# Ordering the gate and up projections of a mixture-of-experts unit: all gate steps ahead of all up steps

## The chip, the cores and the metric

The kernel runs on one core of one Trainium2 chip. The metric is the device time of one execution in microseconds. The kernel before was timed three times, and one more execution was taken with the hardware profiler. All arithmetic that matters here is 32-bit.

## The reference

One inference step of a decoder with two layers, for a prompt of 512 tokens and 8 sampled tokens (520 rows of 1024 features). Each layer adds attention and a convolution branch, and then a mixture of experts. Only the second half is touched by the change:

```python
def hier_moe(h, w_rg, w_re, w_gate, w_up, w_down):
    ...                     # routing: every token gets 2 of 16 experts, all of one group of four
    hg = jnp.einsum('nd,edf->nef', x, w_gate)      # d = 1024, f = 512, e = 16 experts
    hu = jnp.einsum('nd,edf->nef', x, w_up)
    act = jax.nn.silu(hg) * hu * gates[..., None].astype(x.dtype)
    y = jnp.einsum('nef,efd->nd', act, w_down)
```

The kernel computes this sparsely: for each expert it gathers the rows routed to it, up to 128 of them, and adds the result back to those rows.

## The kernel before, in words

**Work and units.** Each layer runs attention, convolution and the output projection, then routing, then the experts. The 16 experts are put in an order by their number of rows. Ten of them form units of their own with 128 places for rows; the last six by size are joined two and two into three paired units (numbers 2, 6 and 11, `PAIRED`), each expert with 64 places. So there are 13 units (`UNITS`), numbered 0 to 12, in each of two layers: 26 in all. `places_of(u)` gives the one or two experts of a unit, and `halves_of(u)` the rows of the tile that each takes. In a paired unit the two experts' matmuls use different halves of TensorE's columns.

**Weights.** Each expert has three weight matrices, gate (j = 0), up (j = 1) and down (j = 2), of 2048 KB each. SyncE loads them into nine slots, in one fixed order (`loads_in_order`, L91): for a single unit gate, up, down; for a paired unit gate and up of the first expert, gate and up of the second, then both downs. Load number n goes to slot n modulo 9 (`slot_of`). Slots 0 to 5 are in the tile `ring`; slot 6 is named `w_last`, 7 `x` and 8 `feat` in the trace, since these tiles are used again. SyncE's loop (L560 to L572) takes the loads strictly in this order; `unit` (L485) waits on `slot_used` of the slot (L489 or L492, L491 being a register step between) until TensorE has made its last use of the previous contents, and then issues the transfer (L493), which adds 16 to `slot_in` when it lands. A load whose slot is not free holds back all loads behind it.

**TensorE** (L971 to L1035) works through the units in an order written out by hand:

```python
for u in range(UNITS):
    if u + 1 < UNITS:
        gate_up(u + 1, range(4))
    turn_hidden(u)
    if u + 1 < UNITS:
        gate_up(u + 1, range(4, KC))
    if u + 2 < UNITS:
        gathered(u + 2)
    down(u)
```

`gate_up(u, ks)` (L971) multiplies the unit's transposed rows `xe_t` with the gate and the up matrix: for each of the 8 chunks k, first gate, then up. Gate results accumulate in PSUM bank 2 or 4, up results in bank 3 or 5, by the unit's parity (banks 2 and 3 are called `pair` in the trace, 4 and 5 `bank`). Ahead of chunk 0 it waits for `xt_ok` (the transposed rows) and for all gate and up loads of the unit (`landed`, L966). Behind chunk 7 stands a matmul of one row and one column (L987) into bank 7 that adds 1 to `gu_ps`; it is called the mark below. The last gate matmul and the last up matmul each give their slot free. `turn_hidden(u)` (L990) transposes the hidden rows of the unit before (4 transposes, L602), `gathered(u + 2)` (L955) transposes the gathered rows of the unit after (8 transposes, L602), and `down(u)` (L996) multiplies by the down matrix and ends with a mark of its own (L1013). For unit 0, `gate_up` is cut into single chunks, with a `unit_list` (L946, small matmuls that make the lists of rows) behind each.

**ScalarE**, for each unit, in this order: `hidden_out(u)` (L1288) copies the transposed hidden rows out of PSUM; `silu(u + 1)` (L1284) waits for `gu_ps` and computes silu of the gate bank into `hid`; `y_half(u)` (L1293) waits for the mark of `down(u)` and scales half of the result.

**VectorE**, for each unit: `hidden(u)` (L1938) waits for `silu_ok` and multiplies `hid` by the up bank (L1408, `v_rows<-v_rows,...`); `features(u + 2)` (L1916) scales the transposed rows of the next unit but one; `y_half(u)` (L1943) waits for the mark of `down(u)` and scales the other half (L1946).

**GpSimd** issues the gather of each unit's rows (L1357) and the scatter-add of its results (L1368).

The functions as they stand in the kernel before:

Of the kernel before, what the change touches and what calls it, by code (L numbers as in the profile page):

```python
# [31 lines left out]
KC = D // P  # L32
# [16 lines left out]
F = 512  # L49
# [9 lines left out]
UNITS = SINGLES + (EXPERTS - SINGLES) // 2  # L59
# [12 lines left out]
def places_of(u):  # L72

    q = u + sum(1 for pair in PAIRED if pair < u)
    return [q, q + 1] if u in PAIRED else [q]
# [15 lines left out]
def loads_in_order():  # L91

    return [(q, j) for u in range(UNITS) for js in ((0, 1), (2,)) for q in places_of(u) for j in js]


def slot_of(q, j):

    return loads_in_order().index((q, j)) % SLOTS_MOE


def load_of(q, j):

    n = loads_in_order().index((q, j))
    return n // SLOTS_MOE + (1 if n % SLOTS_MOE < SLOTS else 0)


def loads_of(s):

    return sum(1 for q, j in loads_in_order() if slot_of(q, j) == s) + (1 if s < SLOTS else 0)
# [85 lines left out]
def hybrid_step(nc, a, o, x_rows, xn_rows):  # L195
# [17 lines left out]
    with ExitStack() as ctx:  # L213
# [3 lines left out]
        def sem(name):  # L217
            return ctx.enter_context(nc.semaphore(name))
# [13 lines left out]
        def cs(name, rows=P):  # L232
            at, width = where[name]
            return const[0:rows, at:at + width]
# [27 lines left out]
        xe_t = probs_flat.rearrange("p (s c n) -> p s c n", s=2, n=P)  # L262
# [64 lines left out]
        bank = [pair_bank[i // 2][:, i % 2, :] for i in range(4)]  # L327
# [7 lines left out]
        slot_used = [sem(f"slot_used{s}") for s in range(SLOTS_MOE)]  # L335
        order_ok = sem("order_ok")
        slots = [ring[:, s, :] for s in range(SLOTS)]
# [89 lines left out]
        xe_in = [sem("xe_in0"), sem("xe_in1")]  # L427
        xt_ps = sem("xt_ps")
        xt_ok = sem("xt_ok")
        gu_ps = sem("gu_ps")  # L430
        silu_ok = sem("silu_ok")
        hid_ok = sem("hid_ok")
# [34 lines left out]
        def halves_of(u):  # L467

            return [slice(0, HALF), slice(HALF, P)] if u in PAIRED else [slice(0, P)]
# [129 lines left out]
        def _(pe):  # L599
            def turn(dst, src, rows):  # L600

                return pe.transpose(dst, src, ident[0:rows, 0:rows])  # L602

            def paired(row, chunk):

                at = (chunk // 2) * 2 * P + chunk % 2
                return row[:, at:at + 2 * P - 1:2]

            pe.wait_ge(start_in, 48)
            with pe.Fori(0, DEPTH) as l:  # L610
# [4 lines left out]
                for c in range(CH):  # L615
                    mm = turn(bank[1][:, c * TAPS:(c + 1) * TAPS], conv_w_rows[:, c * P:(c + 1) * P], TAPS)
                mm.then_inc(vec_ps, 1)

                for t in range(TILES):
                    pe.wait_ge(xn_ok, l * TILES + t + 1)  # L620
                    for g in range(2):
                        b = 4 + 2 * (t % 2) + g
# [4 lines left out]
                        for c in range(4):  # L627
                            mm = turn(bank[b][:, c * P:c * P + rows_of[t]],
                                      x[0:rows_of[t], t, (4 * g + c) * P:(4 * g + c + 1) * P], rows_of[t])
# [4 lines left out]
                for c in range(CH):  # L634
                    if c >= 2:
                        pe.wait_ge(u_ok, l * CH + c - 1)
                    for half in range(2):
# [3 lines left out]
                        for k in range(KC):  # L641
                            w = ring[:, half, k * AW + c * P:k * AW + (c + 1) * P]
                            pe.matmul(main[:, :], w, feat[:, k, 0:SEQ], start=(k == 0), stop=(k == KC - 1))  # L643
                            mm = pe.matmul(smp, w, feat[:, k, SEQ:TOK], start=(k == 0), stop=(k == KC - 1))  # L644
# [10 lines left out]
                for c in range(CH):  # L655
                    for j in range(2):
                        mm = pe.matmul(bank[7][:, c * DEC + 4 * j:c * DEC + 4 * j + 4],
                                       state[:, j, c * P:(c + 1) * P], cs("in_seq", 4 * BUF), start=True, stop=True)
# [273 lines left out]
                for later in range(1, TILES + 1):  # L932
                    mm = pe.matmul(bank[7][:, later * EXPERTS:width + EXPERTS], ones,
                                   chosen[:, 0:(TILES + 1 - later) * EXPERTS], start=False, stop=True,
                                   skip_group_check=True)
# [10 lines left out]
                def unit_list(u):  # L946

                    pe.wait_ge(hot_ok, l * LISTS + FIXED + u + 1)
                    for t in range(TILES):
                        for rows in halves_of(u):  # L950
                            mm = pe.matmul(bank[0][rows, u * PAY:(u + 1) * PAY], hot[:, u % 2, t, rows], pay[:, t, :],
                                           start=(t == 0), stop=(t == TILES - 1))
                    mm.then_inc(idx_ps, 1)

                def gathered(u):  # L955

                    b = u % 2
                    if u >= 2:
                        pe.wait_ge(ht_ok, l * UNITS + u - 1)
                    pe.wait_ge(xe_in[b], l * 16 * len(range(b, UNITS, 2)) + 16 * (u // 2 + 1))  # L960
                    for g in range(2):
                        for c in range(4):
                            mm = turn(bank[6 + g][:, c * P:(c + 1) * P], paired(xe[:, b, :], 4 * g + c), P)
                        mm.then_inc(xt_ps, 1)

                def landed(q, j):  # L966

                    s = slot_of(q, j)
                    pe.wait_ge(slot_in[s], l * 16 * loads_of(s) + 16 * (load_of(q, j) + 1))

                def gate_up(u, ks):  # L971
                    b = u % 2
                    if ks[0] == 0:
                        pe.wait_ge(xt_ok, l * 2 * UNITS + u * 2 + 2)
                        for q in places_of(u):
                            for j in range(2):
                                landed(q, j)
                    for k in ks:
                        for j in range(2):
                            for q, rows in zip(places_of(u), halves_of(u)):  # L980
                                s = slot_of(q, j)
                                mm = pe.matmul(bank[2 + 2 * b + j][rows, :], xe_t[:, b, k, rows],  # L982
                                               slots[s][:, k * F:(k + 1) * F], start=(k == 0), stop=(k == KC - 1))
                                if k == KC - 1:
                                    mm.then_inc(slot_used[s], 1)
                    if ks[-1] == KC - 1:
                        pe.matmul(bank[7][0:1, 0:1], ones[:, 0:1], ones[:, 0:1], start=True, stop=True)\  # L987
                            .then_inc(gu_ps, 1)

                def turn_hidden(u):  # L990
                    pe.wait_ge(hid_ok, l * UNITS + u + 1)
                    for c in range(FC):
                        mm = turn(bank[6][:, c * P:(c + 1) * P], hid[:, u % 2, c * P:(c + 1) * P], P)
                    mm.then_inc(ht_ps, 1)
# [24 lines left out]
                for u in range(FIXED):  # L1019
                    unit_list(u)  # L1020
                for k in range(KC):
                    gate_up(0, range(k, k + 1))
                    unit_list(FIXED + k)
                for u in range(FIXED + KC, UNITS):
                    unit_list(u)
                gathered(1)
                for u in range(UNITS):
                    if u + 1 < UNITS:
                        gate_up(u + 1, range(4))
                    turn_hidden(u)  # L1030
                    if u + 1 < UNITS:
                        gate_up(u + 1, range(4, KC))
                    if u + 2 < UNITS:
                        gathered(u + 2)
                    down(u)  # L1035
# [6 lines left out]
                with pe.If(n_spill > 0):  # L1042
                    pe.wait_ge(y_ok, l * 2 * UNITS + 2 * UNITS + 1)
                    pe.sem_inc(pe_tick, 1)
                    with pe.Fori(0, n_spill) as i:
                        m = pe.snap(before + i)
                        pe.wait_ge(sp_hot, m + 1)
                        for t in range(TILES):
                            mm = pe.matmul(bank[0][:, 0:PAY], hot[:, 0, t, :], pay[:, t, :],
                                           start=(t == 0), stop=(t == TILES - 1))  # L1050
                        mm.then_inc(sp_idx, 1)
                        pe.wait_ge(sp_xe, m * 16 + 16)
                        for g in range(2):
                            for c in range(4):
                                mm = turn(bank[6 + g][:, c * P:(c + 1) * P], paired(xe[:, 0, :], 4 * g + c), P)
# [3 lines left out]
                        for k in range(KC):  # L1059
                            for j in range(2):  # L1060
                                mm = pe.matmul(bank[2 + j][:, :], xe_t[:, 0, k, :], ring[:, j, k * F:(k + 1) * F],
                                               start=(k == 0), stop=(k == KC - 1))
                        mm.then_inc(sp_gu, 1)
                        pe.wait_ge(sp_hid, m + 1)
                        for c in range(FC):
                            mm = turn(bank[6][:, c * P:(c + 1) * P], hid[:, 0, c * P:(c + 1) * P], P)
                        mm.then_inc(sp_ht, 1)
                        pe.wait_ge(sp_htok, m + 1)
                        for k in range(FC):
                            for j in range(2):  # L1070
                                mm = pe.matmul(bank[j][:, :], hid_t[:, 0, k, :],
                                               ring[:, 2, k * D + j * F:k * D + (j + 1) * F],
                                               start=(k == 0), stop=(k == FC - 1))
# [5 lines left out]
        def _(act):  # L1079
# [5 lines left out]
            with act.Fori(0, DEPTH) as l:  # L1085
# [196 lines left out]


                def silu(u):  # L1284
                    act.wait_ge(gu_ps, l * UNITS + u + 1)
                    act.activation(hid[:, u % 2, :], bank[2 + 2 * (u % 2)][:, :], ACT.Silu).then_inc(silu_ok, 1)

                def hidden_out(u):  # L1288
# [4 lines left out]
                def y_half(u):  # L1293
                    act.wait_ge(dn_ps, l * UNITS + u + 1)
                    if u == 0:
# [3 lines left out]
                        .then_inc(y_ok, 1)  # L1299

                silu(0)
                for u in range(UNITS):
                    hidden_out(u)
# [102 lines left out]
        def _(v):  # L1406
            def tt(out, in0, in1, op):
                return v.tensor_tensor(out, in0, in1, op)  # L1408
# [24 lines left out]
            with v.Fori(0, DEPTH) as l:  # L1433
# [26 lines left out]
                for t in range(TILES):  # L1460
                    n = rows_of[t]
                    for g in range(2):
                        v.wait_ge(turn_ps, l * 10 + 2 * t + g + 1)
                        b = bank[4 + 2 * (t % 2) + g][:, :].rearrange("p (c n) -> p c n", c=4)[:, :, 0:n]
# [473 lines left out]
                def hidden(u):  # L1938
                    b = u % 2
                    v.wait_ge(silu_ok, l * UNITS + u + 1)  # L1940
                    tt(hid[:, b, :], hid[:, b, :], bank[3 + 2 * b][:, :], ALU.mult).then_inc(hid_ok, 1)

                def y_half(u):  # L1943
# [106 lines left out]
```

## Time and profile before

| | |
|---|---|
| median of 3 runs | 1523.86 us (1518.89 to 1526.81) |
| the profiled execution, its own time | 1521.59 us |
| its span, first to last instruction | 1519.8 us |
| TensorE busy | 1302.7 us, 86% of the span |
| VectorE / ScalarE / GpSimd busy | 626.5 / 233.3 / 152.4 us |
| mean granted TensorE clock | 0.919 of full speed |
| bytes moved | 318.98 MB, mean 210 GB/s |
| expert units of layer 0 / layer 1, from the first gate matmul to the last down matmul | about 434 to 749 us / 1184 to 1500 us |

"Busy" is the union of an engine's instructions. Each 32-bit matmul shows as two records in the trace, so "x16" at a matmul line is 8 matmuls of a single unit; in a paired unit it is 4 chunks' worth per expert half, and 32 records take the time of 16. PE is TensorE, PEld its weight loads, DVE VectorE, ACT ScalarE, POOL GpSimd, SP SyncE; a "q" behind an engine marks its queue. Names such as `probs`, `v_rows` and `qk_t` are tiles that the expert stage uses again under other names: `xe_t` lies in `probs`, `hid` and `hid_t` in `v_rows`, the gathered rows and `ye` in `qk_t`.

### The profile page before, as it was taken

What the parts mean: (1) busy time and instruction counts of PE and PEld (TensorE: products, weight loads), DVE (VectorE), ACT (ScalarE), POOL (GpSimd) and SP (SyncE); (2) the same over time, 40 slices, a digit from 0 to 9 for tenths busy, and PEclk for the clock granted to TensorE, in tenths of its full rate; (3) what the DMA queues carried; (4) which work ended last, traced back from release to release, by engine and by line L of the source; (5) the groups of instructions that cost most, each with busy time, mean ns of one, the idle gap of its engine ahead of it and who ended that gap; (6) DMA issues with size and microseconds to landing.
All of it is one profiled execution on the core that took longest, in us unless ns stands there. A gap on an engine that the chain in (4) does not pass through costs nothing.

```text
span 1519.8 us, 15302 instructions
## 1 busy us (share of the span) xinstructions
PE 1302.7 (86%) x4730; PEld 629.9 (41%) x4730; DVE 626.5 (41%) x1260; ACT 233.3 (15%) x736; POOL 152.4 (10%) x80
## 2 busy tenths in 40 slices
PE   1999985689769999999649999759895799999994
PEld 1553443445333443444235444335453344444441
DVE  2469988542363111111035799865415611101100
ACT  2002132231100000000020113233211000000000
POOL 0000242000001111110100022400000001101001
PEclk9999997799879999999869999867997799999997
DMA  7800234267355999999384013333742859989973
GB/s 248 309 0 23 70 97 138 67 219 290 113 208 184 357 381 344 374 385 341 63 290 183 0 51 102 92 104 96 285 188 101 309 184 350 386 321 389 388 271 91
DMA packets 102113, 318.98 MB, mean 210 GB/s; under 512 B 10488, under 2 KB 11058, under 8 KB 101932
## 3 DMA queue, kind: packets, MB, share of 16 engines
q1 hardware_dynamic: 84066, 275.49, 48.6%
q0 software_dynamic: 8048, 26.35, 7.2%
q10 hardware_dynamic: 9914, 16.09, 3.2%
q8 instruction: 42, 0.69, 0.2%
q14 instruction: 43, 0.35, 0.1%
HBM read 294.88 MB, written 33.87 MB: 216 GB/s over the span
## 4 chain that ended last, share of the span: by engine, by line
PE 56%; DVE 17%; DMA 12%; DVEq 7%; issue 4%; ACT 1%; ACTq 1%; SPq 1%; POOL 0%; POOLq 0%
PE pair L982 12%; PE pair L1008 9%; PE bank L982 8%; PE pair L643 8%; PE pair L889 8%; DMA w_last<-in_w_up 5%; DVE conv L1504 4%; DVEq L1506 3%; PE bank L602 3%; DMA ring<-in_w_up 3%; DVE probs L1408 2%; DVE sc_dec L1565 2%; DMA x_rows<-qk_t,rows_g 2%; DVE conv L1488 1%; PE pair L762 1%
## 5 line engine op out<-in xcount | busy, mean ns | idle before, releaser
L982 PE MATMUL pair<-ring,probs 128*128 128x512 f32 (+1 forms) x384 | 167.7, 623 | 9.3 <-DMA w_last<-in_w_up 6.9
L1408 DVE TENSOR_TENSOR probs<-bank,vec_g 128x512 f32<-128x512 f32 x52 | 33.5, 685 | 307.2 <-PE bank L602 306.8
L982 PE MATMUL bank<-ring,probs 128*128 128x512 f32 (+1 forms) x352 | 145.0, 606 | 7.7 <-DVE probs L1408 5.6
L643 PE MATMUL pair<-feat,ring 128*128 128x512 f32 x256 | 141.8, 647 | 2.2 <-DVE feat L1408 2.2
L674 PE MATMUL pair<-ring,feat 128*128 128x512 f32 (+1 forms) x320 | 136.9, 606 | 1.6 <-ACT v_rows L1145 1.6
L1008 PE MATMUL pair<-ring,v_rows 128*128 128x512 f32 (+1 forms) x320 | 130.3, 605 | 1.5 <-ACT v_rows L1290 1.5
L1341 POOL TENSOR_TENSOR w_last<-x 128x2048 f32<-128x2048 f32 x16 | 74.0, 4641 | 401.4 <-ACT x L1180 296.2
L1504 DVE SCALAR_TENSOR_TENSOR conv<-u_t,conv_w,conv 128x512 f32<-128x512 f32 x120 | 105.4, 919 | 5.2 <-issue 0.9
L1946 DVE TENSOR_SCALAR qk_t<-pair,gate 128x512 f32<-128x512 f32 x26 | 19.5, 751 | 200.6 <-PE bank L1013 103.5
L1368 POOL DMA_INDIRECT x_rows<-qk_t,rows_g x32 | 49.6, 1552 | 514.4 <-DVE qk_t L1946 468.8
L1488 DVE SCALAR_TENSOR_TENSOR conv<-u_t,conv_w,conv 128x512 f32<-128x512 f32 x120 | 90.2, 751 | 17.3 <-issue 13.2
L982 PEld LDWEIGHTS pair<-ring,probs 128*128 128x128 f32 (+1 forms) x384 | 61.3, 178 | 77.9 <-issue 70.5
L982 PEld LDWEIGHTS bank<-ring,probs 128*128 128x128 f32 (+1 forms) x352 | 57.4, 180 | 80.6 <-issue 79.2
L674 PE MATMUL bank<-ring,feat 128*128 128x512 f32 (+1 forms) x160 | 81.1, 604 | 0.0
L674 PEld LDWEIGHTS pair<-ring,feat 128*128 128x128 f32 (+1 forms) x320 | 50.6, 171 | 73.1 <-issue 72.3
L1008 PEld LDWEIGHTS pair<-ring,v_rows 128*128 128x128 f32 (+1 forms) x320 | 53.1, 183 | 66.0 <-issue 65.8
L644 PEld LDWEIGHTS bank<-feat,ring 128*128 128x128 f32 x256 | 49.5, 194 | 63.2 <-issue 63.2
L1357 POOL DMA_INDIRECT qk_t<-xn_rows,rows_g x26 | 27.3, 1050 | 435.2 <-DVE rows_g L1854 369.3
L889 PE MATMUL pair<-w_last,feat 128*128 128x512 f32 (+1 forms) x160 | 64.8, 592 | 0.0
L889 PE MATMUL pair<-ring,feat 128*128 128x512 f32 (+1 forms) x160 | 64.2, 597 | 0.0
L1008 PE MATMUL pair<-feat,v_rows 128*128 128x512 f32 (+1 forms) x128 | 56.4, 594 | 0.0
L602 PE MATMUL bank<-const,probs 128*128 128x128 f32 x144 | 27.5, 315 | 29.6 <-DVE probs L1639 29.6
(269 smaller groups left out, 1596.2 us busy)
## 6 DMA issues: line engine op xcount, KB each, us to landing
ring<-in_w_gate SPq DMA_DIRECT2D x24, 2048.0 KB, 21.0
ring<-in_w_up SPq DMA_DIRECT2D x22, 2048.0 KB, 21.6
ring<-in_w_down SPq DMA_DIRECT2D x20, 2048.0 KB, 13.2
ring<-in_w_in SPq DMA_DIRECT2D x10, 2048.0 KB, 17.9
x<-in_cache_k SPq DMA_DIRECT2D x64, 256.0 KB, 3.1
x<-in_cache_v SPq DMA_DIRECT2D x64, 256.0 KB, 2.9
feat<-in_w_down SPq DMA_DIRECT2D x8, 2048.0 KB, 20.7
w_last<-in_w_gate SPq DMA_DIRECT2D x6, 2048.0 KB, 15.6
```

Of the source, the lines that this page charges most:

```text
L602: return pe.transpose(dst, src, ident[0:rows, 0:rows])
L643: pe.matmul(main[:, :], w, feat[:, k, 0:SEQ], start=(k == 0), stop=(k == KC - 1))
L644: mm = pe.matmul(smp, w, feat[:, k, SEQ:TOK], start=(k == 0), stop=(k == KC - 1))
L674: mm = pe.matmul(dst[j][rows_at(t, j), :], feat[:, k, cols(t)], ring[:, 2 + j, k * AW:(k + 1) * AW], start=(k == 0), stop=(k == KC - 1))
L889: mm = pe.matmul(bank[2 * (t % 2) + j][rows_at(t, j), :], feat[:, k, cols(t)], w[:, (k % 4) * D + j * AW:(k % 4) * D + (j + 1) * AW], star ...
L982: mm = pe.matmul(bank[2 + 2 * b + j][rows, :], xe_t[:, b, k, rows], slots[s][:, k * F:(k + 1) * F], start=(k == 0), stop=(k == KC - 1))
L1008: mm = pe.matmul(bank[j][rows, :], hid_t[:, b, k, rows], slots[s][:, k * D + j * F:k * D + (j + 1) * F], start=(k == 0), stop=(k == FC - 1))
L1341: pool.tensor_tensor(qk_prod[:, half, :, :], pages[:, half * 4:half * 4 + 4, :], q_rep[:, half:half + 1, :].to_broadcast([P, PAGES, AW]), ...
L1368: pool.indirect_dma_start(out=x_rows[:, :], out_offset=bass.IndirectOffsetOnAxis(ap=rows_g[0:n, at:at + 1], axis=0), in_=ye[0:n, b, :], in ...
L1408: return v.tensor_tensor(out, in0, in1, op)
L1488: v.scalar_tensor_tensor(acc, u_t[:, c, bass.ds(w, SEQ)], conv_w[:, c, bass.ds(w, 1)], acc, ALU.mult, ALU.add)
L1504: v.scalar_tensor_tensor(conv[:, k, 0:SEQ], u_t[:, k, bass.ds(w, SEQ)], conv_w[:, k, bass.ds(w, 1)], conv[:, k, 0:SEQ], ALU.mult, ALU.add)
```

## The change

`gate_up(u, ks)` becomes `gate_or_up(u, j, ks)`, which does the eight chunks of one projection alone. TensorE runs all gate chunks of unit u + 1, then `turn_hidden(u)`, then all up chunks of unit u + 1. Each of the two ends with a mark: the gate's adds to a new semaphore `gate_ps`, the up's to `gu_ps`. The gate part waits for `xt_ok` and for the gate loads, the up part for the up loads. `silu` waits for `gate_ps`; `hidden` on VectorE waits for `silu_ok` and also for `gu_ps`. In unit 0 the eight pieces between the lists are now two gate chunks each for the first four and two up chunks each for the last four. The order of the loads and the waits of SyncE are unchanged.

```diff
+        gate_ps = sem("gate_ps")
         gu_ps = sem("gu_ps")
...
-                def gate_up(u, ks):
+                def gate_or_up(u, j, ks=range(KC)):
                     b = u % 2
                     if ks[0] == 0:
-                        pe.wait_ge(xt_ok, l * 2 * UNITS + u * 2 + 2)
+                        if j == 0:
+                            pe.wait_ge(xt_ok, l * 2 * UNITS + u * 2 + 2)
                         for q in places_of(u):
-                            for j in range(2):
-                                landed(q, j)
+                            landed(q, j)
                     for k in ks:
-                        for j in range(2):
-                            for q, rows in zip(places_of(u), halves_of(u)):
-                                s = slot_of(q, j)
-                                mm = pe.matmul(bank[2 + 2 * b + j][rows, :], xe_t[:, b, k, rows],
-                                               slots[s][:, k * F:(k + 1) * F], start=(k == 0), stop=(k == KC - 1))
-                                if k == KC - 1:
-                                    mm.then_inc(slot_used[s], 1)
+                        for q, rows in zip(places_of(u), halves_of(u)):
+                            s = slot_of(q, j)
+                            mm = pe.matmul(bank[2 + 2 * b + j][rows, :], xe_t[:, b, k, rows],
+                                           slots[s][:, k * F:(k + 1) * F], start=(k == 0), stop=(k == KC - 1))
+                            if k == KC - 1:
+                                mm.then_inc(slot_used[s], 1)
                     if ks[-1] == KC - 1:
                         pe.matmul(bank[7][0:1, 0:1], ones[:, 0:1], ones[:, 0:1], start=True, stop=True)\
-                            .then_inc(gu_ps, 1)
+                            .then_inc(gu_ps if j else gate_ps, 1)
...
                 for k in range(KC):
-                    gate_up(0, range(k, k + 1))
+                    gate_or_up(0, k // 4, range(2 * k % KC, 2 * k % KC + 2))
                     unit_list(FIXED + k)
...
                     if u + 1 < UNITS:
-                        gate_up(u + 1, range(4))
+                        gate_or_up(u + 1, 0)
                     turn_hidden(u)
                     if u + 1 < UNITS:
-                        gate_up(u + 1, range(4, KC))
+                        gate_or_up(u + 1, 1)
...
                 def silu(u):
-                    act.wait_ge(gu_ps, l * UNITS + u + 1)
+                    act.wait_ge(gate_ps, l * UNITS + u + 1)
...
                 def hidden(u):
                     b = u % 2
                     v.wait_ge(silu_ok, l * UNITS + u + 1)
+                    v.wait_ge(gu_ps, l * UNITS + u + 1)
```

## Rows read from the trace of the kernel before

**Rows 1.** Section 2 of the page: busy tenths and granted clock in 40 slices.
```profile
PE   1999985689769999999649999759895799999994
PEclk9999997799879999999869999867997799999997
DMA  7800234267355999999384013333742859989973
```

**Rows 2.** The chain in order of time, unit 6 of both layers: start us, us, what.
```profile
551.59 25.49 DMA w_last<-in_w_up
577.13 8.78 PE pair L982 x32
586.50 7.02 PE pair L982 x32
...
1328.00 8.78 PE pair L982 x32
```

**Rows 3.** Line 982 in a stretch: us, PE busy, PEld busy, clock, DMA share, GB/s.
```profile
577.00:586.00 9.00, 8.78 (x32) 2.61 (x32) 0.81 1.04 355
```

**Rows 4.** TensorE's waits, 430 to 755 us (layer 0): total us, times, longest.
```profile
PE pair L982 <- DMA w_last<-in_w_up: 3.6, 1, 3.6
PE bank L602 <- DVE v_rows L1408: 1.5, 1, 1.5
PE bank L982 <- DMA w_last<-in_w_up: 0.5, 1, 0.5
```

**Rows 5.** TensorE's waits, 1180 to 1505 us (layer 1): total us, times, longest.
```profile
PE pair L982 <- DMA w_last<-in_w_up: 3.3, 1, 3.3
PE bank L982 <- DMA ring<-in_w_up: 0.9, 1, 0.9
PE bank L982 <- DMA w_last<-in_w_up: 0.6, 1, 0.6
PE pair L982 <- DMA ring<-in_w_up: 0.2, 1, 0.2
```

**Rows 6.** TensorE's timeline, unit 4 of layer 0: start us, us, instruction, records.
```profile
534.25 1.02 PE L982 MATMUL pair<-x,probs 128*128 128x512 f32 x2
535.11 0.60 PE L602 MATMUL bank<-const,v_rows 128*128 128x128 f32 x4
...
541.56 1.02 PE L982 MATMUL pair<-x,probs 128*128 128x512 f32 x2
542.51 0.19 PE L987 MATMUL bank<-const 128*1 128x1 f32 x2
542.63 1.23 PE L602 MATMUL bank<-const,qk_t 128*128 128x128 f32 x8
```

**Rows 7.** SyncE's own waits over the whole span: total us, times, longest.
```profile
SPq L492 <- PE pair L1008: 318.7, 22, 30.4
SPq L492 <- PE pair L982: 40.3, 4, 20.1
```

**Rows 8.** Line 493, 550.9 to 551.4 us: second gate load of unit 6, layer 0.
```profile
L493 SPq DMA_DIRECT2D ring<-in_w_gate x1: 373/373/373, 551.0 to 551.0; - x1
DMA to landing us min/median/max: 21.0/21.0/21.0
```

**Rows 9.** Line 493, 574.7 to 575.2 us: gate load of unit 7, layer 0.
```profile
L493 SPq DMA_DIRECT2D ring<-in_w_gate x1: 373/373/373, 574.8 to 574.8; - x1
DMA to landing us min/median/max: 21.3/21.3/21.3
```

**Rows 10.** Line 493, 1302.1 to 1302.7 us: second gate load of unit 6, layer 1.
```profile
L493 SPq DMA_DIRECT2D ring<-in_w_gate x1: 373/373/373, 1302.2 to 1302.2; - x1
DMA to landing us min/median/max: 20.6/20.6/20.6
```

**Rows 11.** VectorE's timeline around the end of a down projection, layer 0.
```profile
528.34 0.75 DVE L1946 TENSOR_SCALAR qk_t<-pair,gate 128x512 f32<-128x512 f32 x1 [6.43 <-PE pair L1013]
529.01 0.68 DVE L1408 TENSOR_TENSOR v_rows<-v_rows,bank 128x512 f32<-128x512 f32 x1
```

## The prediction

> **What bounds the kernel now.** I first read the slices [rows 1]. In both expert stages (the second run of nines in the PE line, and the last) TensorE is busy nine tenths or more almost without a break, at full granted clock but for single slices. The DMA engines are close behind: nine tenths in most of the same slices. So the stage is TensorE's, with a weight supply that has little to spare, and a change pays there only if it takes idle or slow time from TensorE itself. The chain of waits [rows 2] then shows where the supply does win: at unit 6, a paired unit, it leaves TensorE for the transfer of the second up matrix, issued at 551.59 and landed at 577.1. The gate-and-up half behind it takes 8.78 us; the next one, the same work, takes 7.02. TensorE's waits [rows 4, 5] give all such places. In layer 0: 3.6 us (unit 6) and 0.5 (unit 11). In layer 1: 3.3 (unit 6), 0.9, 0.6 and 0.2. Every one of them names an **up** load. That is what the change can act on, since it lets gate chunks run without the up matrix.
>
> **Removed: the waits for up loads.** They sum to 3.6 + 0.5 + 3.3 + 0.9 + 0.6 + 0.2 = 9.1 us. After the change TensorE needs only the gates at that point. At unit 6 of layer 0 it starts at 577.1 after a wait of 3.6 us, so it is ready at 573.5 [rows 2, 4]; the later of the two gates was issued at 551.0 and landed 21.0 us later, at 572.0 [rows 8]. In layer 1 it is ready at 1328.0 − 3.3 = 1324.7 [rows 2, 5], less the 0.9 us saved before it, and the gate landed at 1302.2 + 20.6 = 1322.8 [rows 10]. Both are in time, all the more as the new marks (below) delay TensorE by 6 × 0.21 = 1.3 us up to there. The up chunks follow 7.0 us of gate chunks and 0.6 us of transposes later, about 582 in layer 0, against a landing at 577.1. The other four waits are below 1 us, and 7 us of gate chunks cover them. I take all 9.1 us.
>
> **Removed: slow matmuls behind the idle.** The 8.78 us against 7.02 [rows 2] is the price of the wait in unit 6: TensorE had stood idle 3.6 us, and over its next half the granted clock is 0.81 of full speed [rows 3], a part at 1.2 GHz and the rest at 2.4. That is 1.76 us. Behind the wait of 3.3 us in layer 1 the same half takes 8.78 us too [rows 2], so the same 1.76. The short waits show no such loss that I can separate. Together 3.5 us. Gross gain: 12.6 us.
>
> **Added: a second mark in every unit.** 26 marks (13 units, 2 layers). From the start of the last matmul to the first transpose behind it takes 535.11 − 534.25 = 0.86 us without a mark and 542.63 − 541.56 = 1.07 us with one [rows 6]. A mark thus costs 0.21 us of TensorE, not hidden by anything, and 26 cost 5.5 us. The lower bound is the step from mark to transpose alone, 542.63 − 542.51 = 0.12 us or 3.1 us in all; the upper one is 0.25 us each, 6.5 in all, since readings to 0.01 us at four places may be off by 0.04. I take 5.5, since it is measured between the very neighbours that the new mark gets. The Trainium skill, "TensorE: Matmul & The Clock Gate", section "Back-to-back issue gap", puts a matmul of 1 to 64 columns at about 25 ns when warm; a mark of two records would then cost an estimated 0.05 us, 26 of them 1.3 us, and the net gain would be 11.3 us. The row above disagrees with that.
>
> **Moved: the order of the matmuls.** Gate and up alternated between two PSUM banks; now 8 chunks in a row accumulate in one bank. No row shows two such instructions in a row. The nearest is inside one matmul: its two records go to the same bank, and end 1.02 us after its start, while the next instruction starts after 0.86 [rows 6]. At an even pace that is a record every 0.43 us, each 1.02 − 0.43 = 0.59 long, overlapping the next by 0.16 us within a bank as between banks. No turnaround shows, so I take zero; the upper bound is a rival below. The number of weight loads is the same, each record having its own before and after. A gain is excluded, as the matmuls already follow at their streaming rate.
>
> **Moved: when slots come free.** The gate slots are freed some 7.6 us earlier, one half of the unit. But SyncE issues strictly in order, and it hardly ever waits for gate-and-up: 318.7 us over 22 waits stand on down (L1008), 40.3 us over 4 on L982, two of them 20 us long [rows 7]. Those two are the first reuse of unit 0's gate slot in each layer, by a load of unit 2 that TensorE reaches only after all of unit 1, and the load behind it needs the up slot, free as late as before. I cost this at nothing. The up slots are freed 0.21 us later per mark, already in the sum. No DMA issue is moved on any queue, and POOL's gathers and scatters depend on events (`xt_ps`, `y_ok`) behind the same work as before.
>
> **Moved: silu.** It can start about 7.7 us earlier. Its consumer, the multiply, stands on VectorE behind `y_half` of the unit before, which waits for that unit's down: the L1946 row is followed at once by the multiply [rows 11]. Down comes after both gate and up, so the multiply starts when it did. The same holds at the end of a layer, where TensorE's 1.5 us wait for the multiply [rows 4] stays. Worth nothing. The new wait of VectorE on `gu_ps` is long satisfied there. Behind TensorE's wait for the up loads stand the gather's transposes and down, hence SyncE's next load; with 5 us to spare in unit 6 nothing of it is late.
>
> **What is late next.** TensorE reaches unit 7 sooner while the loads already queued do not. From unit 6's first chunk to unit 7's, TensorE now needs 8.78 + 7.02 us of gate and up [rows 2], 7.0 of down (as many matmuls as one half) and 0.6 + 1.2 of transposes [rows 6], 24.6 in all; without the slow part and with one more mark it is 23.0 us, so from 574.8 (573.5 + 1.3) it ends at 597.8. Unit 7's gate, issued at 574.8, lands at 596.1 [rows 9]: 1.7 us to spare. The loads behind it are issued at the end of down and move forward with TensorE.
>
> **The sum.** −9.1 − 3.5 + 5.5 = −7.1 us against the profiled 1521.59, giving 1514.5 there. The median of the three runs stands 2.3 us above the profiled execution, so the predicted median is 1523.86 − 7.1, or 1516.8 us.
>
> **The rivals.**
>
> 1. *The mark is cheaper.* If most of its 0.21 us is overlap that the next instruction takes back, the lower bound of 3.1 us holds and the gain is 9.5: 1514.4 us. For it: the two readings are of one unit, and the transposes on either side differ in their tiles. Against it: both intervals run between starts of real work, with no wait in them. Chance 0.16.
>
> 2. *The waits move instead of going.* The supply has only 1 to 3 us to spare at units 6 and 7. If the gates land late there, TensorE idles again and its clock may fall again. With 1 us of idle and 1.76 us of slow chunks back in each layer, 5.5 us of the gain is lost: 1522.3 us. For it: the DMA line at nine [rows 1], landings that depend on gathers beside them. Against: both gates were down before TensorE arrived [rows 8, 10]. Chance 0.20.
>
> 3. *Accumulating in one bank costs a turnaround,* the rival on the slower side. Its place is each of the 14 same-bank neighbours of a unit: 24 units × 14, and 8 in each of the two units 0, 352 in all. If each had to let the one before drain, it would lose that overlap of 0.16 us, 56 us in all: 1573 us. It decides from 7.1 / 352 = 20 ns per neighbour; 42 ns make it slower by over 0.5%. For it: these pairs are in no row. Against: the two records of a matmul pay nothing. Chance 0.06.
>
> 4. *The change does not do what it says.* The gate does not in fact start early, since something else holds it (the rows' `xt_ok`, or a gate that lands last). Then only the marks remain: 1529.4 us. Rows 8 and 10 speak against it. Chance 0.04.
>
> **How the numbers follow.** The forecast has the remaining 0.54. A measurement of this kernel can tell about 0.5%, 7.6 us, from no change, so "faster" is below 1516.2 and "slower" above 1531.5. The forecast value lies almost on the first line: of its 0.54 I give 0.25 to faster, 0.29 to same. Rival 1 gives 0.14 and 0.02; rival 2 0.02 and 0.18; rival 3 0.01 to same and 0.05 to slower; rival 4 0.03 to same and 0.01 to slower. That is 0.41 faster, 0.53 same, 0.06 slower. The range starts below rival 1 by the spread that three runs show (1518.89 is 5 us under the median), less part of it since it is a median: 1511.0. It reaches past rival 2: 1523.5. That leaves out rivals 3 and 4 and the tails.
>
> **What would show it.** Right: TensorE's waits on `in_w_up` in the expert stages are gone or below 0.5 us; both halves of unit 6 take about 7.0 us; 52 marks instead of 26 on gate and up; from the last gate matmul to the transposes 1.07 us; the L1946 row still followed at once by the multiply; SyncE's waits still on down. Wrong: waits on `in_w_gate` in units 6 to 9 and a clock that falls again there (rival 2); gate chunks further than 0.86 us apart (rival 3); a multiply that starts ahead of `y_half`, which would give silu's early start a value that I deny it.

## The result, and the profile after

| | before | changed |
|---|---|---|
| median, 8 runs each | 1523.14 us (1518.55 to 1526.81) | 1513.31 us (1508.68 to 1517.11) |
| ratio of the two, 95% interval | | 0.9935, 0.9918 to 0.9952 |
| the profiled execution, own time / span | 1521.59 / 1519.8 us | 1517.11 / 1515.3 us |
| mean granted TensorE clock, profiled | 0.919 | 0.914 |

The change is worth 9.8 us on the medians, 0.65%; the interval reaches from 7.3 to 12.5 us. The forecast was 1516.8 us in a range of 1511.0 to 1523.5, a gain of 7.1. The profiled execution of the changed kernel is the slowest of its eight, so the two spans are only 4.5 us apart; lengths below are therefore compared stage by stage. The mean clock of the profiled execution is not higher either: it rises in the expert stages (0.97 to 0.98) and is lower in the first 435 us (0.91 to 0.89), which the change does not touch.

The slices of the page, same three lines as [rows 1]:

```profile
PE   1999986799868999999649999858896799999994
PEclk9999996599969999999969999966997799999997
DMA  8800234177363999999375012332752849999973
```

The picture is the same: TensorE and the DMA engines are both near nine tenths in the expert stages. It can't show what changed. TensorE's waits can. Layer 0 (430 to 755 us), the answer to [rows 4]; the columns are total us, times, longest:

```profile
PE bank L603 <- DMA qk_t<-xn_rows,rows_g: 6.7, 1, 6.7
PE bank L982 <- DVE probs L1408: 3.0, 1, 3.0
PE pair L952 <- DVE conv L1408: 1.7, 3, 0.9
PE bank L603 <- DVE v_rows L1408: 1.5, 1, 1.5
PE pair L982 <- DVE probs L1408: 1.0, 1, 1.0
PE pair L1008 <- ACT v_rows L1290: 0.8, 1, 0.8
```

This is the whole list, and no weight load is in it (idle below 0.15 us is not listed). Layer 1's list has none either: all 9.1 us of [rows 4, 5] are gone. The wait of 1.5 us for the multiply in the last unit is still there, as forecast.

The chain at unit 6 of layer 0, the answer to [rows 2]; start us, us, what:

```profile
574.91 2.58 PE pair L1008 x6
577.48 0.12 PE pair L1013 x2
577.61 7.02 PE pair L982 x32
584.62 0.12 PE bank L987 x2
584.74 0.59 PE bank L603 x4
585.33 7.02 PE pair L982 x32
592.35 0.12 PE bank L987 x2
```

No DMA is in the chain, down is followed by the gate chunks at once, and both halves take 7.02 us where the first took 8.78. The granted clock over that stretch (here line 982 in 577 to 586 us, columns as [rows 3]) is 1.00 where it was 0.81:

```profile
577.00:586.00 9.00, 7.83 (x36) 2.55 (x38) 1.00 1.04 382
```

The marks, the answer to [rows 6], from TensorE's timeline in unit 4 of layer 0:

```profile
531.72 7.13 PE L982 MATMUL pair<-w_last,probs 128*128 128x512 f32 x16
538.79 0.19 PE L987 MATMUL bank<-const 128*1 128x1 f32 x2
538.91 0.66 PE L603 MATMUL bank<-const,v_rows 128*128 128x128 f32 x4
539.40 7.03 PE L982 MATMUL pair<-x,probs 128*128 128x512 f32 x16
546.36 0.19 PE L987 MATMUL bank<-const 128*1 128x1 f32 x2
546.48 1.23 PE L603 MATMUL bank<-const,qk_t 128*128 128x128 f32 x8
```

Eight chunks in one bank take 7.03 us, as eight alternating ones did: no turnaround. The transposes start 1.07 us behind the start of the last gate matmul, as forecast (eight chunks at 0.86 us: the last one starts at 537.84). But the chunks behind them follow after 539.40 − 538.91 = 0.49 us. In the kernel before it was 535.55 − 535.11 = 0.44, by [rows 6] and the row that follows there:

```profile
535.55 1.02 PE L982 MATMUL pair<-w_last,probs 128*128 128x512 f32 x2
```

So 0.05 us of a mark's price stands behind the transposes, where the forecast did not look.

SyncE still waits on down, 296.3 us over 22 waits, and 41.6 us over 4 on gate and up: the gate slots that come free earlier start no load earlier that TensorE waits for.

```profile
SPq L493 <- PE pair L1008: 296.3, 22, 30.7
SPq L493 <- PE pair L982: 41.6, 4, 13.4
```

The next load, unit 7's gate (line 494, 578.7 to 579.2 us, the answer to [rows 9]):

```profile
L494 SPq DMA_DIRECT2D ring<-in_w_gate x1: 373/373/373, 578.9 to 578.9; - x1
DMA to landing us min/median/max: 21.0/21.0/21.0
```

It landed at 599.9 and TensorE asked for it at 600.5. I had given it 1.7 us to spare; it had 0.6. The working had delayed TensorE by the new marks but left the issue at its old time, 574.8. The issue follows the end of unit 5's down by 1.4 us in both kernels (573.4 and 574.8 before, 577.5 and 578.9 here), so it moves with the marks too.

The same length of work can be read between the ends of two units' down matmuls in the timelines. In us, layer 0 / layer 1; "with unit 6" is the stretch that holds unit 6's gate and up, "last two units" runs from the end of down of unit 10 to that of unit 12, and the expert stage from the first gate matmul to the end of the last down:

```
kernel                          single unit   with unit 6      last two units   expert stage
before, first profile           22.64         28.29 / 27.92    33.57 / 33.81    315.1 / 316.9
before, second profile          22.64         28.85 / 27.63    33.58 / 33.72    317.5 / 316.8
changed, first profile          22.91         23.01 / 23.01    32.10 / 33.79    311.7 / 312.9
changed, second profile         22.91         23.01 / 23.01    32.10 / 32.10    311.8 / 311.9
```

### The profile page after: what moved, and what is told of

It is laid out like the page before. It is cut to its first block, busy times and chain, and to the rows that moved or that the text cites. A ratio compares the mean times of both kernels' runs of the same rounds, so it can differ in the third digit from the quotient of the medians.

```text
span 1515.3 us, 15414 instructions
## 1 busy us (share of the span) xinstructions
PE 1312.0 (87%) x4782; PEld 632.1 (42%) x4782; DVE 626.7 (41%) x1260; ACT 230.4 (15%) x736; POOL 152.5 (10%) x80
## 4 chain that ended last, share of the span: by engine, by line
PE 64%; DVE 17%; DVEq 7%; DMA 4%; issue 4%; ACT 1%; ACTq 1%; SPq 0%; POOL 0%; POOLq 0%
PE pair L982 13%; PE bank L982 11%; PE pair L1008 11%; PE pair L644 8%; PE pair L890 8%; PE bank L603 4%; DVE conv L1504 4%; DVEq L1506 3%; DVE probs L1408 2%; DVE sc_dec L1565 2%; DMA x_rows<-qk_t,rows_g 2%; DVE conv L1488 1%; PE pair L763 1%; PE pair L766 1%; DVE u_t L1408 1%
## 5 line engine op out<-in xcount | busy, mean ns | idle before, releaser
L982 PE MATMUL pair<-ring,probs 128*128 128x512 f32 (+1 forms) x384 | 163.2, 611 | 1.9 <-DVE probs L1408 1.9
L1408 DVE TENSOR_TENSOR probs<-bank,vec_g 128x512 f32<-128x512 f32 x52 | 33.5, 685 | 299.7 <-PE bank L603 299.3
L1298 ACT ACTIVATE qk_t<-pair,gate 128x512 f32<-128x512 f32 x26 | 17.9, 687 | 355.2 <-PE pair L1013 187.2
```

## The experiments

Each kernel is timed against the kernel before on the same chip; ratios are to it.

**e4_before_again and e7_changed_again: second profiles.** No edit.

> The kernel before once more, for a second profile of it. I forecast a gain of 7.1 us from the first profile and 9.8 was measured on the medians. If the first profile showed smaller waits than usual, this one shows more than 9.1 us of TensorE's waits for up loads; if not, 9 us again, and the rest is in the clock or in other stages.

> The changed kernel once more, for a second profile. If the stage of the experts again takes 311 to 313 us in each layer with no wait for a load, then the changed kernel's steady length is known and the rest of the difference lies in how long the kernel before waits; if the last unit again takes 32.1 us in layer 0 against 33.5 before, that part is the change's too and not chance.

Measured: the second profile of before has TensorE waiting 4.2 and 1.0 us in layer 0, 3.0, 1.2 and 0.6 in layer 1 for up loads:

```profile
PE pair L982 <- DMA w_last<-in_w_up: 4.2, 1, 4.2
PE bank L982 <- DMA w_last<-in_w_up: 1.0, 1, 1.0
```

That is 10.0 us against 9.1, so the first profile was a little mild. The second profile of the changed kernel has no wait for a load. Two profiles each give expert stages of 633.1 us before and 624.2 after, both layers together: 9.0 us, close to the 9.8 of the medians. These two second profiles are single executions (1526.21 and 1517.53 us). The last two units are 1.5 to 1.7 us shorter in three of four stages of the changed kernel.

**e3_gate_waits_for_up: everything but the early start.**

```diff
                         for q in places_of(u):
                             landed(q, j)
+                            if j == 0:
+                                landed(q, 1)
```

> The changed kernel, but the gate chunks wait for the up loads too. Everything else (order of the matmuls, two marks, silu on the gate's mark, gate slots freed early) is as in the changed kernel. Theory: the waits come back (unit 6: 3.5 less 1.8 us of marks ahead of it, so about 2 us in each layer, with or without slow chunks behind), and the time is that of the kernel before with two marks: 1525 to 1527 us, ratio 1.002. Rival (the gain is from the order, from silu or from slots freed early): 1513 us, ratio 0.9935.

Measured: 1524.36 us, ratio 1.0012 (0.9997 to 1.0027). The waits are back, here layer 0's:

```profile
PE pair L984 <- DMA w_last<-in_w_up: 3.2, 1, 3.2
PE bank L984 <- DMA ring<-in_w_up: 0.3, 1, 0.3
```

This one added wait undoes the whole gain. Order, silu on the gate's mark and the earlier freeing of gate slots are all still in, and are worth nothing together that these runs can see. I had expected about 2 us of wait at unit 6, from 3.5 less the marks ahead of it; it was 3.2 and 2.5.

**e2_before_two_marks: the marks alone.**

```diff
+        gate_ps = sem("gate_ps")
...
-                    if ks[-1] == KC - 1:
+                    if ks[-1] in (KC // 2 - 1, KC - 1):
                         pe.matmul(bank[7][0:1, 0:1], ones[:, 0:1], ones[:, 0:1], start=True, stop=True)\
-                            .then_inc(gu_ps, 1)
+                            .then_inc(gu_ps if ks[-1] == KC - 1 else gate_ps, 1)
```

> The kernel before with a second mark, for which nothing waits, behind chunk 3 of every gate-and-up. Theory: 26 x 0.26 = 6.8 us more work on TensorE, of which the waits for up loads at unit 6 swallow the 7 marks ahead of them in each layer (3.6 us): 1523.1 + 3.2, about 1526.3 us, ratio 1.002; single units 22.9 us. Rival (a mark is nearly free): ratio 1.000, single units 22.65 us.

Measured: 1524.38 us, ratio 1.0016 (1.0002 to 1.0029); single units take 22.91 us, and unit 6 waits 2.9 and 2.6 us. The marks cost what their number says, and part of it disappears in the waits, which are shorter than in the kernel before. e2 and e3 give the same time: with the same marks and the same waits, alternating banks or not makes no difference beyond their intervals of about 2 us each way. So the turnaround is at most about 10 ns for each of the 352 neighbours, and the chunks' 7.03 us in both orders leave less.

**e1_one_mark: the early start without its mark.**

```diff
-                    if ks[-1] == KC - 1:
+                    if ks[-1] == KC - 1 and j == 1:
                         pe.matmul(bank[7][0:1, 0:1], ones[:, 0:1], ones[:, 0:1], start=True, stop=True)\
-                            .then_inc(gu_ps if j else gate_ps, 1)
+                            .then_inc(gu_ps, 1)
...
-                    act.wait_ge(gate_ps, l * UNITS + u + 1)
+                    act.wait_ge(gu_ps, l * UNITS + u + 1)
...
-                    v.wait_ge(gu_ps, l * UNITS + u + 1)
```

> The changed kernel without the gate's mark; silu waits for gu_ps again, as before the change. Theory (the gain is the early start of the gate chunks, the mark is a pure cost, silu's early start is worth nothing): a single unit in the changed profile takes 22.91 us against 22.64 before, so a mark costs 0.26 us, 26 of them 6.8 us; this kernel should take 1513.3 - 6.8 = 1506.5 us, ratio to before 0.989, with no wait of TensorE for an up load. Rival (silu's early start carries part of the gain): 1513 us or more, ratio 0.9935 or above.

Measured: 1510.45 us, ratio 0.9907 (0.9888 to 0.9926). By the ratios it is 4.3 us faster than the changed kernel, between my 6.8 and the rival's nothing. Single units are back at 22.64 us. Two things took the rest. A first wait for a gate load shows, unit 7's, 0.2 us in layer 0 and 0.3 in layer 1:

```profile
PE bank L982 <- DMA ring<-in_w_gate: 0.2, 1, 0.2
```

And the last two units took 33.5 us in both layers, not 32.1.

**e5_silu_on_slot: silu early, without a mark.**

```diff
-                    act.wait_ge(gate_ps, l * UNITS + u + 1)
+                    for q in places_of(u):
+                        act.wait_ge(slot_used[slot_of(q, 0)], used_after(q, 0, l))
```

The gate's mark is left out as in e1_one_mark, so TensorE's part is the same; `used_after` is the number that the slot's semaphore has reached after that load's last use.

> The changed kernel without the gate's mark, but with silu still early: it waits for the semaphore by which the last gate matmul frees its slot. TensorE does what it does in e1_one_mark, and only silu's start differs. Theory (silu's early start is worth nothing, since the multiply stands behind y_half on VectorE): the time of e1_one_mark within noise, ratio 0.990 to 0.991, and the multiply starts 0.7 us after y_half as before. Rival (silu's early start gains something): 0.988 or lower.

Measured: 1510.35 us, ratio 0.9912 (0.9892 to 0.9931), the same as e1_one_mark. The timelines show why. ScalarE's silu of one unit (L1293; start us, us):

```profile
533.93 0.59 ACT L1293 ACTIVATE v_rows<-pair 128x512 f32<-128x512 f32 x1
```

and the next two rows of VectorE that matter:

```profile
548.67 0.75 DVE L1954 TENSOR_SCALAR qk_t<-pair,gate 128x512 f32<-128x512 f32 x1 [6.28 <-PE bank L1019]
549.34 0.68 DVE L1415 TENSOR_TENSOR v_rows<-v_rows,pair 128x512 f32<-128x512 f32 x1
```

silu is done at 534.5, and the multiply that uses it starts at 549.3, straight behind `y_half` (L1954), which waited for the mark of down. The 15 us between are idle for the result.

**e6_no_marks: no marks at all.** As e5_silu_on_slot, and

```diff
-                    if ks[-1] == KC - 1:
-                        pe.matmul(bank[7][0:1, 0:1], ones[:, 0:1], ones[:, 0:1], start=True, stop=True)\
-                            .then_inc(gu_ps if j else gate_ps, 1)
...
-                    pe.matmul(bank[2 + 2 * b][0:1, 0:1], ones[:, 0:1], ones[:, 0:1], start=True, stop=True)\
-                        .then_inc(dn_ps, 1)
...
-                    v.wait_ge(dn_ps, l * UNITS + u + 1)
+                    for q in places_of(u):
+                        v.wait_ge(slot_used[slot_of(q, 2)], used_after(q, 2, l))
```

with the same replacement in the multiply (load 1), in ScalarE's `y_half` (load 2) and in SyncE's wait ahead of a spill.

> As e5_silu_on_slot, and the marks of up and of down are gone too: the multiply and both y_half wait for the slot semaphores that the last up and last down matmul add to. Theory: a mark costs about 0.26 us, so a single unit takes 22.1 us instead of 22.64 and 52 marks are worth 13 us. But one mark less per unit already made TensorE wait 0.2 to 0.3 us for the gate of unit 7; 7 units x 0.53 us sooner must meet that load again, so 2.5 to 4 us of wait for a gate load come back in each layer, perhaps with slow chunks behind them. Net 3 to 8 us below e1_one_mark: 1503 to 1507 us, ratio 0.985 to 0.989. Rival (marks are free, or the supply follows): ratio 0.991, or 0.982 with no wait.

Measured: 1502.56 us, ratio 0.9855 (0.9834 to 0.9877), a version that beats both kernels. Single units take 21.99 us. The supply is met where I said, in layer 0 at units 7 and 6:

```profile
PE bank L988 <- DMA ring<-in_w_gate: 1.3, 1, 1.3
PE pair L988 <- DMA ring<-in_w_gate: 1.1, 1, 1.1
```

and in layer 1 for 1.3 and 0.4 us. That is 2.4 and 1.7 us in the two layers, a little less than the 2.5 to 4 I had expected. With 4.1 us of wait in all, no slow chunks follow: unit 7's first half shows 7.13 us in the timeline.

```profile
598.61 7.13 PE L988 MATMUL bank<-ring,probs 128*128 128x512 f32 x16 [1.28 <-DMA ring<-in_w_gate]
```

**e9_before_no_marks: no marks, old order.** The same replacements in the kernel before.

> The kernel before (gate and up chunk by chunk, all loads waited for ahead of them) without its 52 marks, the waits taken from the slot semaphores as in e6_no_marks. Theory (the supply at unit 6 limits this order): single units take 22.1 us, but the marks ahead of unit 6, 6 units x 0.5 us, are given back there as a longer wait for the up load, 6 to 7 us in each layer instead of 3.5; also more wait in units 11 and 3. Of 13 us some 6 to 8 are kept: 1515.5 to 1517.5 us, ratio 0.995 to 0.996, that is, about 12 us above e6_no_marks although both lack all marks. Rival (supply is no limit): ratio 0.991.

Measured: 1521.62 us, ratio 1.0004 (0.9988 to 1.0020). I expected to keep 6 to 8 of the 13 us; the interval leaves room for 1.8 us at most. TensorE's waits in layer 0:

```profile
PE pair L988 <- DMA w_last<-in_w_up: 4.7, 1, 4.7
PE bank L988 <- DMA w_last<-in_w_up: 2.8, 1, 2.8
PE bank L988 <- DMA ring<-in_w_up: 1.1, 1, 1.1
PE pair L988 <- DMA ring<-in_w_up: 0.7, 1, 0.7
```

and 8.2 us in layer 1: 17.5 us in all against 9.1 in [rows 4, 5]. The clock falls further too. Around unit 6 of both layers, columns as [rows 3], first the kernel before (line 982), then this one (line 988); these windows hold the wait as well:

```profile
573.00:583.00 10.00, 5.87 (x20) 1.89 (x22) 0.83 1.04 370
1324.00:1334.00 10.00, 6.00 (x20) 1.89 (x22) 0.83 1.04 373
573.00:583.00 10.00, 3.73 (x10) 1.25 (x12) 0.68 1.03 385
1322.00:1332.00 10.00, 5.62 (x16) 1.77 (x18) 0.66 1.04 358
```

The stretch with unit 6 takes 29.5 us where the same work without waits takes 22.65 (e8_gates_first): 4.7 us of wait and 2.1 behind it. The one with unit 11's gate and up takes 27.2 us in layer 0. Added up over the ten stretches from the end of unit 0's down to the end of unit 10's, both layers, this kernel takes 469.6 us and the kernel before 467.6 and 468.5 (two profiles): nothing of the marks' time is kept there. Its expert stages as a whole are 628.7 us, 4.4 less than before, and the last two units are 4.2 us shorter (31.4 and 31.7 us; more on these below); the timed runs do not show these 4.4 us, and why is open.

**e8_gates_first: both gates of a pair loaded first.** As e6_no_marks, and

```diff
-    return [(q, j) for u in range(UNITS) for js in ((0, 1), (2,)) for q in places_of(u) for j in js]
+    return [(q, j) for u in range(UNITS) for js in ((0,), (1,), (2,)) for q in places_of(u) for j in js]
```

> As e6_no_marks, and the loads of a paired unit come in the order gate, gate, up, up, down, down, so that TensorE's first part needs the first two loads of the unit and not the first and third. Theory: e6_no_marks waits 1.1 and 0.4 us for the second gate of unit 6, and this wait goes; the 1.3 us in each layer for the gate of unit 7 stays or grows by what was saved, since it stands behind all six loads of unit 6. So 0 to 2 us below e6_no_marks: ratio 0.984 to 0.986. Rival (the order of loads decides all waits): all waits for gates gone, ratio 0.982.

Measured: 1501.65 us, ratio 0.9881 (0.9856 to 0.9906), its interval overlapping that of e6. I had expected 0.984 to 0.986, below e6; no gain over e6 is shown, and the two ratios are from different chips. The wait at unit 6 is gone and the one at unit 7 has taken it up:

```profile
PE bank L988 <- DMA ring<-in_w_gate: 2.5, 1, 2.5
```

in layer 0, 1.5 us in layer 1: 4.0 us in all, as in e6. The order of the six loads moved the wait and did not shorten it; the rival (0.982) falls.

## Why the prediction was right, and where its sum was off

The sign, the mechanism and the size held: 9.8 us measured, 7.1 forecast, the time inside the range. The number is nearer to the cheap mark's 1514.4 than to the forecast's 1516.8, but not for that rival's reason. Two terms were mis-sized by about half a microsecond in opposite directions, which cancel by luck, and the rest of the difference is a term that the sum did not have. Step by step:

- **The waits for up loads go, 9.1 us.** Right, and shown by e3_gate_waits_for_up: put back the one wait and the gain is gone. The term is 9.1 in one profile and 10.0 in the other.
- **The slow chunks behind them, 3.5 us.** Right: 8.78 against 7.02 us, clock 0.81 against 1.00.
- **26 marks, 5.5 us.** Slightly low. A single unit goes from 22.64 to 22.91 us, 0.27 us a mark, and only 0.12 in the three stretches with a paired unit's gate and up (22.89 us in e1_one_mark, 23.01 in the changed kernel): 2 × (10 × 0.27 + 3 × 0.12) = 6.1 us. The part that was missing is the 0.05 us behind the transposes, shown above. The estimate of 0.05 us that the prediction worked out from the Trainium skill ("TensorE: Matmul & The Clock Gate", "Back-to-back issue gap") is out by a factor of five here.
- **Order of banks, slots freed early, silu early: nothing.** Right (e2 against e3, e3, e5 against e1).
- **What the sum left out.** The last down of layer 0. In the changed kernel it runs at full clock and takes 7.13 us:

```profile
738.82 0.66 PE L603 MATMUL bank<-const,v_rows 128*128 128x128 f32 x4 [1.53 <-DVE v_rows L1408]
740.24 7.13 PE L1008 MATMUL pair<-ring,v_rows 128*128 128x512 f32 x16 [0.76 <-ACT v_rows L1290]
```

  The kernel before has the same two idle times there, 1.53 and 0.76 us, and its last down takes 8.82 us:

```profile
739.19 0.66 PE L602 MATMUL bank<-const,v_rows 128*128 128x128 f32 x4 [1.53 <-DVE v_rows L1408]
740.60 8.82 PE L1008 MATMUL pair<-ring,v_rows 128*128 128x512 f32 x16 [0.76 <-ACT v_rows L1290]
```

  I had called this part unchanged, since its waits are. The waits are; the clock behind them is not. By the means of the two profiles each the last two units are 33.67 and 32.52 us, 1.15 us per layer or 2.3 in all, unit 12's new mark already paid. Which kernels have it:

```
kernels                                     marks per unit   last down at full clock    last two units
before, e1_one_mark, e5_silu_on_slot        2                0 of 8 layers              33.5 to 33.8
changed, e3, e2                             3                6 of 8 layers              32.1 (33.8 in the other two)
e6_no_marks, e8_gates_first                 0                0 of 4 layers              33.1 to 33.2
e9_before_no_marks                          0                2 of 2 layers              31.4 and 31.7
```

  (Each profile has two layers; the marks of down are counted.) So it goes neither with the early start, which e2 and e3 lack, nor with the order of the chunks. Among kernels with marks it comes with the third one, but e9 has it with none. The kernel before, e1, e6 and the changed kernel show the same two idle times ahead of it, 1.5 to 1.6 and 0.8 us. I read it as a matter of the moment at which the idle falls, which no run isolates. It isn't a part of what the early start is worth: e2 and e3 have it in three of four layers and are no faster than the kernel before.

With these the sum is 9.6 (the mean of the two profiles' waits) + 3.5 + 2.3 − 5.6 (the marks without unit 12's) = 9.8 us. The stretch from the first gate matmul to the end of unit 0's down, marks apart, was 0.5 us longer per layer in the changed kernel (49.9 us against 48.9, of which two marks are 0.5), 1.0 in all, but the four stages of before differ there by 1.5 us among themselves, so I don't count it as the change's. With it the sum is 8.8 us, against 9.0 from the expert stages and 9.8 from the medians. The other stages, which the change doesn't touch, differ by up to 3 us each among the four profiles; that is why 4.5 us in the spans is no measure of the change.

Of the rivals, the cheap mark is wrong, its price being above the forecast and not below. The wait that moves to a gate did not appear, but was nearer than I said: one mark less per unit, 1.6 us by unit 7, brought it in (e1). The issue moves forward with TensorE, but the landing does not follow in full: unit 7's gate of layer 0 lands 21.0 us behind its issue in the changed kernel, 21.7 in e1 and 23.6 in e6. The turnaround is nothing: chunks follow at 0.86 us in both orders. That the change does nothing is excluded.

## What to carry to other kernels

Where a consumer waits for two transfers before it starts, and can do half its work with the first, split the wait; the order of the loads need not change. Save time on the engine and widen the supply together: here taking the 52 marks out of the old order was worth nothing beyond the noise (1.0004), taking the 78 out of the new order another 0.8% (0.9855 against 0.9935), because only the new order could take its weights later (17.5 us of waits for loads against 4.1). And a semaphore that another instruction already raises at the right moment is cheaper than a small instruction that exists to raise one.

## What the runs showed of the hardware that I had not expected

- A one-column matmul that serves as a mark costs 0.27 to 0.33 us between large ones: 22.91, 22.64 and 21.99 us for a unit with three, two and none. Its records show where it goes: TensorE's weight loader is idle 0.77 us ahead of each mark (mean of 52), against 0.26 us ahead of a weight load of line 982 into `pair` (mean of the 374 that have such a gap). From the list of waits of the changed kernel:

```profile
PEld pair L982 <- issue: 97.4, 374, 1.1
PEld bank L987 <- issue: 40.1, 52, 0.8
```

  In the timeline of the weight loader the first transpose's load of the kernel before (without a mark) starts at 534.68, with the last record of the large matmul ahead of it, and waits 0.43 us for its turn. The mark's load starts at 538.78, 0.52 us behind the start of that last record and together with the mark itself:

```profile
534.68 0.14 PEld L602 LDWEIGHTS bank<-const,v_rows 128*128 128x128 f32 x1 [0.24 <-issue]
538.78 0.09 PEld L987 LDWEIGHTS bank<-const 128*1 128x1 f32 x2 [0.76 <-issue]
```

  So the mark's weights are not loaded early, as those of a transpose are; why was not tried.
- The price of a wait is more than its length and not in proportion to it. Behind 1.3 us (e6) the chunks were at full speed. 2.5 us cost 0.3 more in layer 0 of e8_gates_first (the stretch of unit 7 took 24.9 us, against 22.1 without a wait in e9_before_no_marks), but in layer 1 of e3_gate_waits_for_up the stretch with unit 6 took 27.0 us, 4.0 more than the 23.01 without a wait. 3.0 to 4.2 us in the two profiles of the kernel before cost 1.7 to 1.8 more. 4.7 and 4.8 us cost 2.1 and 2.4 more (e9), at a granted clock of 0.68 and 0.66 around them. One length of wait, 2.5 us, thus has two prices here; what decides between them no run isolates.
